# Halves of the rotated features exchanged by small loads in chip memory instead of a product with a permutation

## The chip, the cores and the metric

One core of one Trainium2 chip runs the whole program in one launch. The time is the device time of that launch in microseconds (us). TensorE multiplies, VectorE and ScalarE work on tiles, GpSimd does small work beside them, and SP (the sync engine) issues all loads and stores. Everything is float32; the large products are made in three passes from rounded parts.

## What is computed

Three layers on 512 positions of 1,024 features: an attention over a sliding window of 128 with one sink per head, a stick-breaking attention, and a hybrid mixer (convolution and state space), each with a gated feed-forward part. The change concerns the first attention, of 16 query heads and 2 key heads of 64 features:

```python
q = partial_rope(rmsnorm(q, q_gain), positions)
k = partial_rope(rmsnorm(k, k_gain), positions)
...
x1, x2 = xr[..., :half], xr[..., half:]
rot = jnp.concatenate([x1 * cos - x2 * sin, x2 * cos + x1 * sin], axis=-1)
return jnp.concatenate([rot, x[..., ROT_DIM:]], axis=-1)
```

Only the first 16 of the 64 features of a head are turned (`half` is 8), so every turned feature needs the one that stands 8 further on or back.

## The kernel before

Features lie on the 128 partitions, positions (512) along the row. A query tile holds two heads, at partitions 0 to 63 and 64 to 127; there are eight query tiles and one tile of keys, "k". `score()` writes one list of steps (ticks), and every engine runs through the same list and does its own part of each step, in that order, so the order of work is written out by hand. Signals (semaphores) tie the engines together; `Waits.wait_ge` leaves out waits that are already known to hold.

Weights come as a stream of 361 units of 512 KB (eight blocks of 128 by 128): SP loads one into one of three `raw` buffers (L1892) once VectorE is done with the unit that was there, ScalarE makes its upper part (`cut`, L1128), VectorE its lower part (L1420), and TensorE makes three products for each block (L755, L757, L759). Beside it SP loads the modulation weights (L1905, 512 KB each, six buffers), and VectorE multiplies and adds them (L1428, L1431); such a load waits for the multiply-add that frees its buffer.

The first attention, 66 to 176 us of the profiled execution, is a pipeline woven into the products of the queries' own projection and, later, of the output projection. For a tile `t`, the step `query` (for the keys `kstat` and `krope`) does this:

- ScalarE, when the product of the tile is done: square into `QSQ`, and the tile times its gain into `QG` (L1208, L1209), one of five buffers.
- TensorE: sums of squares (`head_stats`, L876), then the product of `QG` with a permutation matrix, which exchanges rows 0 to 7 with 8 to 15 and rows 64 to 71 with 72 to 79 and leaves zero elsewhere (`turn_halves`, L884), each into a bank of its own.
- VectorE: the statistics out of the bank (L1601), `QG` times the cosines (L1611), the permuted tile times the signed sines into `qt` (L1615), and the sum (L1617). GpSimd takes the power -1/2 of the statistics (L1833).

For the keys, `kspread` spreads the statistics over the rows (L902) and VectorE scales the keys with it (L1622); the values are transposed (L910). Then the pipeline has four stages for each half of a tile: `scores` (L927; VectorE adds the mask and takes maxima, L1645), `exps` on ScalarE (L1287), `turned` (transposes, L941) and `values` (L955, L965, then L1672 on VectorE). In one round the list has `scores` of a new half, `query` of the next tile, and the later stages of earlier halves.

The eight banks of PSUM are handed round in turn: `take` pops the bank that was given longest ago and waits for what was to be done with it, `give` puts it back at the end of the row. From `query` of tile 6 on, four of the eight are held by results of the output projection.

```python
def take(key):
    i, sig, by = free.popleft()
    if sig is not None:
        w.wait_ge(sig, by)
    bank_of[key] = i
    return psum[i]
```

## Time and profile before

| | |
|---|---|
| median of 3 runs | 2362.5 us (2361.22 to 2362.77) |
| profiled execution | 2362.4 us |
| its span | 2360.6 us |
| TensorE busy | 2302.7 us (98%) |
| VectorE busy | 1168.1 us (49%) |
| ScalarE busy | 870.8 us (37%) |
| GpSimd busy | 155.1 us (7%) |
| mean granted clock of TensorE | 0.991 |

The span runs from the first to the last instruction of the profiled execution; its own time also has what lies around the span. A busy TensorE is not a TensorE at its peak, since matmuls overlap and their ends are modelled; starts are safer than ends. A wait is shown with the instruction behind it and with what ended it. The granted clock is a share of 2.4 GHz.

### The profile page before, as it was taken

The numbers are of one execution on the slowest core, as the hardware profiler recorded it, in microseconds if no ns is written. First come the engines' busy times: TensorE is split into PE (matmuls) and PEld (weight loads), VectorE is DVE, ScalarE is ACT, GpSimd is POOL, SyncE is SP. The second block draws the span as 40 slices with busy tenths as digits, with TensorE's granted clock in tenths as the row PEclk, the third lists the DMA queues.
The fourth block names the chain that finished last, engine by engine and source line by source line (L and its number), as shares of the span: only waits on it lengthen the run. The fifth ranks groups of instructions, "written<-read, shape, count | busy, mean of one in ns | idle before, by whom it ended". The sixth has DMA issues, their size and how long they took to land.

```text
span 2360.6 us, 27446 instructions
## 1 busy us (share of the span) xinstructions
PE 2302.7 (98%) x11216; PEld 1842.1 (78%) x11216; DVE 1168.1 (49%) x1615; ACT 870.8 (37%) x1413; POOL 155.1 (7%) x145
## 2 busy tenths in 40 slices
PE   8999999999999999999999999999999999999998
PEld 6767788888777677888887877866778887888886
DVE  3765665543465744333335455556743345553453
ACT  3554322132354533322323236356363223332332
POOL 1111000000100010000010002022020001000001
PEclk9999999999999999999999999999999999999999
DMA  9323465522212122222232222211223222233222
GB/s 318 134 99 111 175 216 202 207 98 98 81 63 72 46 71 83 96 98 98 90 107 81 98 90 98 98 55 63 72 90 107 98 81 98 87 101 106 92 88 81
DMA packets 77518, 250.69 MB, mean 106 GB/s; under 512 B 8272, under 2 KB 16720, under 8 KB 77392
## 3 DMA queue, kind: packets, MB, share of 16 engines
q1 hardware_dynamic: 77392, 248.93, 30.4%
q8 instruction: 89, 1.46, 0.3%
q14 instruction: 37, 0.30, 0.0%
HBM read 244.70 MB, written 4.19 MB: 105 GB/s over the span
## 4 chain that ended last, share of the span: by engine, by line
PE 82%; ACT 3%; DVE 3%; issue 1%; POOL 1%; POOLq 0%; DVEq 0%; ACTq 0%
PE pb L755 25%; PE pb L759 24%; PE pb L757 24%; PE pb L979 1%; PE pb L1004 1%; PE pb L989 1%; PE pb L1073 1%; DVE slab L1684 1%; PE pb L779 1%; PE pb L775 1%; PE pb L777 1%; PE pb L1054 1%; PE pb L800 0%; PE pb L861 0%; ACT slab L1381 0%
## 5 line engine op out<-in xcount | busy, mean ns | idle before, releaser
L755 PE MATMUL pb<-hhi,whi 128*128 128x512 f32 x1976 | 787.0, 398 | 4.2 <-ACT hhi L1156 2.4
L1420 DVE TENSOR_TENSOR wlo<-raw,whi 128x1024 fp32r<-128x1024 f32 x361 | 449.1, 1248 | 686.9 <-ACT whi L1128 686.9
L757 PE MATMUL pb<-hhi,wlo 128*128 128x512 f32 x1976 | 771.3, 390 | 1.7 <-DVE wlo L1420 1.7
L759 PE MATMUL pb<-hlo,whi 128*128 128x512 f32 x1976 | 771.4, 390 | 0.4 <-DVE hlo L1416 0.4
L1128 ACT ACTIVATE whi<-raw 128x1024 fp32r<-128x1024 f32 x361 | 379.2, 1056 | 688.8 <-PE pb L759 672.0
L755 PEld LDWEIGHTS pb<-hhi,whi 128*128 128x128 f32 x1976 | 371.2, 188 | 98.5 <-issue 24.5
L759 PEld LDWEIGHTS pb<-hlo,whi 128*128 128x128 f32 x1976 | 371.2, 188 | 81.8 <-DVE hlo L1416 1.6
L757 PEld LDWEIGHTS pb<-hhi,wlo 128*128 128x128 f32 x1976 | 371.7, 188 | 78.8 <-DVE wlo L1420 2.7
L755 PE MATMUL pb<-ahi,whi 128*128 128x512 f32 x848 | 336.2, 396 | 1.4 <-ACT ahi L1310 0.7
L759 PE MATMUL pb<-alo,whi 128*128 128x512 f32 x848 | 331.3, 391 | 0.0
L757 PE MATMUL pb<-ahi,wlo 128*128 128x512 f32 x848 | 331.2, 391 | 0.0
L755 PEld LDWEIGHTS pb<-ahi,whi 128*128 128x128 f32 x848 | 159.9, 189 | 39.2 <-issue 6.1
L759 PEld LDWEIGHTS pb<-alo,whi 128*128 128x128 f32 x848 | 159.7, 188 | 34.5 <-DVE alo L1416 0.8
L757 PEld LDWEIGHTS pb<-ahi,wlo 128*128 128x128 f32 x848 | 159.9, 189 | 32.7 <-issue 0.7
L1842 POOL TENSOR_TENSOR slab<-slab 128x512 f32<-128x512 f32 x44 | 62.0, 1410 | 1588.2 <-ACT slab L1145 1587.3
L1511 DVE SCALAR_TENSOR_TENSOR slab<-slab,vec 128x509 f32<-128x509 f32 (+2 forms) x132 | 99.0, 750 | 4.7
L1416 DVE TENSOR_TENSOR alo<-slab,ahi 128x512 fp32r<-128x512 f32 x90 | 62.3, 692 | 67.9 <-ACT ahi L1227 50.4
L1431 DVE SCALAR_TENSOR_TENSOR slab<-slab,small 128x1024 f32<-128x1024 f32 x70 | 89.9, 1284 | 1.9
L1145 ACT ACTIVATE slab<-X 128x512 f32<-128x512 f32 x48 | 30.3, 632 | 109.3 <-PE pb L759 39.5
L1684 DVE TENSOR_TENSOR_SCAN slab<-slab,cst 128x128 f32<-128x128 f32 (+3 forms) x64 | 52.5, 820 | 31.0 <-ACT slab L1323 31.0
L1542 DVE TENSOR_TENSOR slab<-slab,pb 128x512 f32<-128x512 f32 x66 | 45.0, 682 | 43.6 <-PE pb L759 43.6
L1227 ACT ACTIVATE ahi<-slab 128x512 fp32r<-128x512 f32 x66 | 41.7, 632 | 66.0 <-DVE slab L1542 65.8
(232 smaller groups left out, 1702.9 us busy)
## 6 DMA issues: line engine op xcount, KB each, us to landing
raw<-stream SPq DMA_DIRECT2D x361, 512.0 KB, 3.3
slab<-ada_w SPq DMA_DIRECT2D x80, 512.0 KB, 5.0
early<-ada_w SPq DMA_DIRECT2D x32, 256.0 KB, 7.6
X<-xT SPq DMA_DIRECT2D x8, 256.0 KB, 4.5
ya<-slab SPq DMA_DIRECT2D x8, 256.0 KB, 2.3
slab<-ya SPq DMA_DIRECT2D x8, 256.0 KB, 4.9
outT<-X SPq DMA_DIRECT2D x8, 256.0 KB, 2.1
cst<-consts SPq DMA_DIRECT2D x1, 576.0 KB, 7.2
```

What stands on the lines that cost most here:

```text
L755: e.matmul(out, wh, hi, start=s.k == 0, stop=False)
L757: e.matmul(out, wl, hi, start=False, stop=False)
L759: i = e.matmul(out, wh, lo, start=False, stop=s.last)
L1128: e.activation(whi[:, u % NW, :], raw[:, u % NRAW, :], ACT.Copy).then_inc(*a_cut.up(u))
L1227: e.activation(a_out[f % HALF][0], SG[f % 6], ACT.Copy).then_inc(*a_half.up(("f", l, f)))
L1416: e.tensor_tensor(out, src, hi.bitcast(F), ALU.subtract).then_inc(*v_half.up(key))
L1420: e.tensor_tensor(wlo[:, u % NW, :], raw[:, u % NRAW, :], whi[:, u % NW, :].bitcast(F), ALU.subtract).then_inc(*v_cut.up(u))
L1431: e.scalar_tensor_tensor(o, a, cond[:, k:k + 1], o, ALU.mult, ALU.add).then_inc(*v_mod.up(("fma", n)))
L1511: e.scalar_tensor_tensor(t[:, d:], u[:, :S - d], W(name, (width - 1 - d) * tiles + i), t[:, d:], ALU.mult, ALU.add).then_inc(*v_conv.up((k ...
L1542: e.tensor_tensor(t, t, b, ALU.mult).then_inc(*v_ev.up(tile))
L1684: e.tensor_tensor_scan(p[:, 0:wd][:, ::-1], RS[n % 4][:, 0:wd][:, ::-1], C("late", S - wd)[:, 0:wd][:, ::-1], 1.0, ALU.mult, ALU.max).then ...
L1842: e.tensor_tensor(acc, acc, sq_of(sid, d), ALU.add).then_inc(*p_sum.up((sid, d)))
```

## The change

The product with the permutation goes, with its bank, for all nine tiles. In its place a buffer `swapped` (slot 46, which the first attention did not use) is cleared once by GpSimd, and SP fills its 32 rows that matter with four loads from `QG`, eight rows of 2 KB each, at the steps `krope` and `query`. Before it issues them SP waits for the clearing, for ScalarE's `QG`, and for VectorE's product with the sines of the tile before, which reads the same buffer. VectorE's product with the sines waits for the fourth load and reads `swapped` in place of the bank. The order of work on VectorE stays.

```diff
+    d_swap = signal("d_swap", 16)
...
-    qt = slot(21)
+    qt, swapped = slot(21), slot(46)
...
-        def turn_halves(t):
-            b = take(("rope", t))
-            w.wait_ge(d_late, "in")
-            w.wait_ge(a_ev, ("qkv", qn(t) + 7 if t == "k" else t) if t != "k" else ("qkv", 8))
-            e.matmul(b, C("perm"), QG[qn(t) % 5], start=True, stop=True).then_inc(*t_att.up(("rope", t)))
-            give(("rope", t), v_att, ("rope2", t))
...
-        def query(t):
-            head_stats(t)
-            turn_halves(t)
...
-            w.wait_ge(t_att, ("rope", t))
+            w.wait_ge(d_swap, (t, 3))
             if t != "k":
                 w.wait_ge(v_att, ("rope", t - 1 if t else "k"))
-            e.tensor_tensor(qt, bank(("rope", t)), sinT, ALU.mult).then_inc(*v_att.up(("rope2", t)))
+            e.tensor_tensor(qt, swapped, sinT, ALU.mult).then_inc(*v_att.up(("rope2", t)))
...
+        def tables():
+            w.wait_ge(t_mod, ("pre", 3))
+            e.memset(swapped, 0.0).then_inc(*p_rope.up("blank"))
...
+        def swap(t):
+
+            w.wait_ge(p_rope, "blank")
+            w.wait_ge(a_ev, ("qkv", 8 if t == "k" else t))
+            if t != "k":
+                w.wait_ge(v_att, ("rope2", t - 1 if t else "k"))
+            for n, (to, of) in enumerate(((0, 8), (8, 0), (64, 72), (72, 64))):
+                e.dma_start(swapped[to:to + 8, :], QG[qn(t) % 5][of:of + 8, :]).then_inc(*d_swap.up((t, n)))
...
-        do = {"cut": lambda u: load() if u > 2 else None, "fma": fma, "evac": evac, "fetch": fetch, "final": final}
+        do = {"cut": lambda u: load() if u > 2 else None, "fma": fma, "evac": evac, "krope": lambda: swap("k"), "query": swap, "fetch": fetch, "final": final}
```

SP's queue around the keys and the first tiles, before: L1892 loads a unit of the weight stream, L1905 modulation weights.

```order
L1892 DMA raw<-stream 128x1024 [waits v_cut]
L1905 DMA slab<-ada_w 128x1024 [waits v_mod] x4
L1892 DMA raw<-stream 128x1024 [waits v_cut] x2
L1905 DMA slab<-ada_w 128x1024 [waits v_mod] x2
L1892 DMA raw<-stream 128x1024 [waits v_cut]
L1905 DMA slab<-ada_w 128x1024 [waits v_mod]
```

The same place with the change: L1886 and L1899 are these two lines, L1914 is the exchange (`spare_74` is `swapped`).

```order
L1899 DMA slab<-ada_w 128x1024 [waits v_mod] x4
L1914 DMA spare_74<-slab 8x512 [waits a_ev,p_rope]
L1914 DMA spare_74<-slab 8x512 x3
L1914 DMA spare_74<-slab 8x512 [waits v_att,a_ev]
L1914 DMA spare_74<-slab 8x512 x3
L1886 DMA raw<-stream 128x1024 [waits v_cut]
L1914 DMA spare_74<-slab 8x512 [waits v_att,a_ev]
L1914 DMA spare_74<-slab 8x512 x3
L1886 DMA raw<-stream 128x1024 [waits v_cut]
L1899 DMA slab<-ada_w 128x1024 [waits v_mod] x2
L1914 DMA spare_74<-slab 8x512 [waits v_att,a_ev]
L1914 DMA spare_74<-slab 8x512 x3
```

The exchanges of the keys and of tile 0 stand behind four loads of modulation weights, that of tile 1 behind one load of the stream, that of tile 2 behind one of the stream and two of modulation weights; the next load of the stream comes behind each.

TensorE at the same place, before: two sums of squares (L876), each with a permutation (L884), between products of the projection.

```order
L759 MATMUL pb<-hlo,whi 128x512
L876 MATMUL pb<-cst,slab 128x2 x4
L884 MATMUL pb<-slab,cst 128x512
L876 MATMUL pb<-cst,slab 128x2 x4
L884 MATMUL pb<-slab,cst 128x512
L755 MATMUL pb<-hhi,whi 128x512
L757 MATMUL pb<-hhi,wlo 128x512
L759 MATMUL pb<-hlo,whi 128x512
```

And with the change (L877 is L876; L756, L758 and L760 are L755, L757 and L759):

```order
L760 MATMUL pb<-hlo,whi 128x512
L877 MATMUL pb<-cst,slab 128x2 x8
L756 MATMUL pb<-hhi,whi 128x512
L758 MATMUL pb<-hhi,wlo 128x512
L760 MATMUL pb<-hlo,whi 128x512
```

The two statistics stand together and the products of the projection follow at once.

## Rows read from the trace of the kernel before

**Rows 1.** Page, part 4: shares of the chain that ended last, by engine.

```profile
PE 82%; ACT 3%; DVE 3%; issue 1%; POOL 1%; POOLq 0%; DVEq 0%; ACTq 0%
```

**Rows 2.** Busy time by stretches; at the end clock, DMA share, GB/s.

```profile
50.00:100.00 50.00, 47.22 (x265) 34.92 (x264) 37.81 (x86) 24.60 (x53) 8.03 (x4) 0.97 0.50 177
100.00:150.00 50.00, 50.00 (x397) 38.63 (x396) 32.81 (x109) 33.95 (x91) 6.03 (x3) 1.00 0.24 86
150.00:200.00 50.00, 42.03 (x305) 32.02 (x305) 26.00 (x81) 25.98 (x73) 4.02 (x2) 0.93 0.24 85
```

**Rows 3.** Line of the permutation: min/median/max ns, first and last start.

```profile
L884 PE MATMUL pb<-slab,cst x16: 592/634/676, 67.8 to 174.5; 128*128 128x512 f32 x16
```

**Rows 4.** TensorE in order of time: start, us, engine, line, operation.

```profile
75.47 1.93 PE L902 MATMUL pb<-cst,small 128*64 128x128 f32 x16 [2.78 <-POOL small L1833]
...
81.45 0.93 PE L927 MATMUL pb<-slab 64*128 64x128 f32 x8
...
85.17 0.95 PE L876 MATMUL pb<-cst,slab 128*128 128x2 f32 x8
85.99 1.10 PE L884 MATMUL pb<-slab,cst 128*128 128x512 f32 x2
87.02 1.14 PE L927 MATMUL pb<-slab 64*128 64x256 f32 x8
```

**Rows 5.** VectorE in order of time, the start of the attention.

```profile
67.80 5.44 DVE L1431 SCALAR_TENSOR_TENSOR slab<-slab,small 128x1024 f32<-128x1024 f32 x4
73.16 0.16 DVE L1601 TENSOR_SCALAR small<-pb 128x8 f32<-128x8 f32 x1
...
73.84 0.68 DVE L1615 TENSOR_TENSOR slab<-pb,slab 128x512 f32<-128x512 f32 x1
...
77.44 0.69 DVE L1622 TENSOR_TENSOR slab<-slab,pb 128x512 f32<-128x512 f32 x1 [0.19 <-PE pb L902]
```

**Rows 6.** SP's issues in order of time: start us, us, how many.

```profile
1.64 0.42 SPq L1928 DMA_DIRECT2D pos<-positions  x1
...
68.29 3.93 SPq L1905 DMA_DIRECT2D slab<-ada_w  x4
...
92.86 0.91 SPq L1905 DMA_DIRECT2D slab<-ada_w  x2
...
135.16 0.81 SPq L1905 DMA_DIRECT2D slab<-ada_w  x2
...
153.80 0.43 SPq L1905 DMA_DIRECT2D slab<-ada_w  x1
```

**Rows 7.** DMA issues, KB each, us to landing: 82:88, then 0:20.

```profile
raw<-stream SPq DMA_DIRECT2D x1, 512.0 KB, 3.1
...
pos<-positions SPq DMA_DIRECT2D x1, 2.0 KB, 2.3
```

**Rows 8.** Stretches of half a us, then DMA strips of 92:100 and 153:159.

```profile
76.50:77.00 0.50, 0.50 (x10) 0.50 (x6) 0.47 (x2) 0.00 (x0) 0.50 (x1) 0.50 0.85 344
77.00:77.50 0.50, 0.50 (x5) 0.17 (x2) 0.31 (x2) 0.00 (x0) 0.42 (x1) 0.50 0.21 82
...
DMA  0000000974999998999989998989521000000000
...
DMA  0000000008979989999999989685432100000000
```

**Rows 9.** VectorE's product with the sines, tiles 2, 5 and 6.

```profile
96.62 0.69 DVE L1615 TENSOR_TENSOR slab<-pb,slab 128x512 f32<-128x512 f32 x1
...
139.93 0.68 DVE L1615 TENSOR_TENSOR slab<-pb,slab 128x512 f32<-128x512 f32 x1
...
155.19 0.68 DVE L1615 TENSOR_TENSOR slab<-pb,slab 128x512 f32<-128x512 f32 x1
```

**Rows 10.** TensorE's first products with the values, tiles 4 and 5; wait in brackets.

```profile
157.69 1.55 PE L955 MATMUL pb<-slab 128*64 128x128 f32 x12 [1.10 <-DVE small L1645]
...
177.65 0.88 PE L955 MATMUL pb<-slab 128*64 128x128 f32 x12 [0.45 <-DVE small L1645]
```

More of the change, by code:

```diff
@@ L1085, in tensor @@
               "tables": tables, "kstat": lambda: head_stats("k"),
-              "krope": lambda: turn_halves("k"), "kspread": kspread, "vturn": vturn, "query": query, "scores": scores, "turned": turned,
+              "kspread": kspread, "vturn": vturn, "query": head_stats, "scores": scores, "turned": turned,
               "values": values, "start": start, "turn": turn, "gather": gather, "dtturn": dtturn, "xrow": xrow, "bturn": bturn,
@@ L1872, in decay @@
             e.tensor_tensor(ex[:, P:], ex[:, P:], Ct[g % 2][:, P:], ALU.mult).then_inc(*p_ssd.up(("ex", g, h)))
-        do = {"angles": angles, "pow": pow_, "kstat": lambda: head_pow("k"), "query": head_pow, "sq": sq,
+        def tables():
+            w.wait_ge(t_mod, ("pre", 3))
+            e.memset(swapped, 0.0).then_inc(*p_rope.up("blank"))
+        do = {"angles": angles, "tables": tables, "pow": pow_, "kstat": lambda: head_pow("k"), "query": head_pow, "sq": sq,
               "evac": evac, "state": state, "decay": decay}
@@ L1946, in program @@
     engines = tensor, scalar, vector, gpsimd, sync
-    signals = [d_in, d_pos, d_out, *d_x, *d_raw, *d_ada, *d_early.values(), d_late, *d_ya, t_mm, t_mod, t_norm, t_att, t_stick, t_ssd, a_cut, a_half,
+    signals = [d_in, d_pos, d_out, *d_x, *d_raw, *d_ada, *d_early.values(), d_late, d_swap, *d_ya, t_mm, t_mod, t_norm, t_att, t_stick, t_ssd, a_cut, a_half,
                a_ev, a_sq, a_att, a_stick, a_ssd, v_cut, v_half, v_ev, v_mod, v_norm, v_res, v_att, v_stick, v_ssd, v_conv, p_sum,
```

## The prediction, made before the changed kernel had run

> **What bounds the kernel now.** The page first. The chain of waits that ended last is 82% TensorE [rows 1], so what counts is time in which TensorE works or waits. The change touches only the attention of the first layer, 66 to 176 us, so I read busy time by stretches next: TensorE is busy 50.00 of 50 us from 100 to 150, but only 42.03 from 150 to 200 [rows 2]. In the middle, a product less is time gained. At the two ends of the pipeline TensorE waits for others, and there it is not. The granted clock says the same: 1.00 in the middle, 0.97 and 0.93 around it. Since its two levels are 2.4 and 1.2 GHz, 0.97 of 50 us is 3.0 us at half clock and 0.93 is 7.0 us; one dip costs about 1.5 us of work.
>
> Then the line that goes. Nine products with the permutation take two passes of some 0.63 us each [rows 3] (eight of them; the ninth reads another buffer). What one occupies is read from starts: the one of tile 1 starts at 85.99, the scores behind it at 87.02, so 1.03 us [rows 4].
>
> **The change, part by part.** Time runs from the profiled execution, 2362.4 us for a span of 2360.6; the median of the three runs is 2362.5, so the same.
>
> Removed, tiles 1 to 5: five products of 1.03 us in the stretch without idle time, 5.15 us gained if the new wait stays hidden.
>
> Removed, keys and tile 0: nothing. After them TensorE waits 2.78 us at 75.47 for GpSimd's power of the key statistics [rows 4], and that hangs on VectorE, which is busy with multiply-adds (5.44 us from 67.80) and takes the key statistics only at 73.16 [rows 5]. Two products less make this wait 4.8 us instead of 2.8. The half clock behind it (0.50, [rows 8]) is there already.
>
> Added: 36 loads of 8 rows by 2 KB on SP, four for each tile, and VectorE's wait for the fourth. No row shows such a load. An issue is bounded by nothing below and by 0.42 us above, which the 2 KB of positions took [rows 6]; I take 0.42, since a load of as few bytes took it. Landing: 2.3 us for that one, 3.1 us for a 512 KB weight load alone [rows 7]; I take 2.3 and keep 2.0 to 3.8 for the range, the upper end because writes from chip memory to chip memory have no row. So a quartet lands 3 x 0.42 + 2.3 = 3.56 us after SP gets to it, at best.
>
> When SP gets to it is the second question. SP is released by VectorE's splits and multiply-adds, so before each exchange it has just issued one to four loads of 512 KB, which stand ahead of it in the same queue.
>
> Keys: SP has issued its fourth modulation load by 68.29 + 3.93 = 72.22 [rows 6]; by itself the exchange would land at 75.8. But the transfers ahead run until about 77.2: share 0.85 and then 0.21 in two half microseconds [rows 8]. I take 77.4. VectorE wanted the turned keys at 73.84 [rows 5]. Tile 0's exchange may start only when the product with the sines of the keys is done (one buffer for all), 0.69 us later at 78.1, and lands at 78.1 + 3.56 = 81.65. Behind it stand that product, the sum and the scaling of the keys, with the pitches of the trace 0.72 + 0.60 + 0.69 = 2.0, so the keys are ready at 83.65 where they were at 77.44 + 0.69 = 78.13 [rows 5]. TensorE wants them at 81.45 [rows 4], as now, since its order up to there starts from 75.47. Stall: 83.65 - 81.45 = **+2.2 us**.
>
> Tile 2: SP is free at 92.86 + 0.91 = 93.77 [rows 6], three loads of 512 KB ahead run out at about 98.0 [rows 8], in the first strip with slices of 0.2 us, so the exchange lands at 98.2 and VectorE wanted it at 96.62 [rows 9]. It waits 1.6 us, but has some microseconds of slack behind it; for TensorE 0, at most 1.
>
> Tile 5, the closest of the others: free after the first of the two loads, which share 0.81 us from 135.16, at 135.58 [rows 6] (the second now comes behind the exchange), landing 139.1 against 139.93 [rows 9]. Hidden. Tiles 1, 3, 4 and 7 have 1 us or more.
>
> Tile 6: SP free at 153.80 + 0.43 = 154.23 [rows 6]; transfers ahead end at about 157.4 [rows 8], in the second strip with slices of 0.15 us, own landing 157.8. VectorE wanted it at 155.19 [rows 9], so everything behind it on VectorE comes 2.6 us later, the score maxima of tile 5 first. TensorE stands at exactly these: the bank for the output of tile 4 comes free with them, and it waits for that until 157.69 [rows 10]. With the banks handed round in turn and two takings fewer a tile, this bank's releaser stays the same. So **+2.6 us**, and the saved product is only more waiting. At tile 7 the same pair stands a little apart (wait 0.45 us [rows 10], exchange long landed): about 0.2 gained.
>
> GpSimd's one clearing of the buffer lies long before 72 us. VectorE's product reads chip memory instead of a bank: same duration within 0.01 us. Bytes: 9 x 64 KB, nothing beside 512 KB loads.
>
> Sum: 2.2 - 5.15 + 2.6 - 0.2 = -0.55 us, **2361.9 us**.
>
> The row for positions is a load on an idle queue. The Trainium skill, "DMA: Bandwidth & Descriptors", section "Anatomy of one DMA", gives 2.0 us fixed plus bytes over 436 GB/s for one transfer, fitted for another way of issuing, so an estimate of 2.04 us here. By that price in place of 2.3 the exchanges of tile 0 and tile 6 land 0.26 us sooner (that of the keys waits for the transfers ahead all the same), and the sum would be -1.1 us.
>
> **Rivals.** (a) *The exchange does not queue behind the large loads.* For it: 8 rows need not travel over the same engines as 128. Then the exchange of the keys lands at 75.8, the product behind it ends at 76.5, that of tile 0 lands at 80.1, the keys are ready at 82.1, stall 0.65; tile 6 unchanged, since its own 3.56 us decides. Sum -2.1 us: 2360.3. Against it: a 512 KB load behind another takes longer to land, as its transfers come in turn. The Trainium skill, same page, section "Queues, rings and completion order", says that each engine consumes one ring's descriptors in ring order; by that rule (a) falls, and the sum stays -0.55.
>
> (b) *Issues of 8 rows cost 0.1 us and land in 2.0 us.* Then 2.3 us in place of 3.56 each time: keys 74.5, tile 0 at 77.5, no stall at the start, tile 6 late by 1.35. Sum -5.15 + 1.35 - 0.2 = -4.0: 2358.4. If tile 6 is hidden as well, -5.35: 2357.0, the most that can be had. Against it: positions took 0.42 us although tiny.
>
> (c) *The exchange becomes the wait*, on the slow side. If four chip-memory loads land in 3.8 us instead of 2.3, tile 0's comes 1.5 us later, the stall before the first scores is 3.7 us, longer than the wait of 2.78 us after which the clock is at half [rows 4, 8]. That is 1.5 us, and 1.5 more for a dip. Tile 6 pays 1.5 more, tiles 3 and 5 pass their margins for some 0.7. Sum -0.55 + 5.2 = +4.65: 2367.0, and more with each further tenth. For it: two exchanges in series stand at the start with nothing between them, and the dependence on one buffer. It decides from a landing of about 3.8 us.
>
> **How the numbers follow.** A measurement of this kernel tells 0.2%, 4.7 us, from no change. Chances: forecast 0.45, (a) 0.20, (b) 0.15, (c) 0.20. Forecast and (a) are within the bound; (b) goes past it about half of the time, and so does (c) with most of its chance: faster 0.10, same 0.71, slower 0.19. The range runs from just below (b), 2358.0, to just past the edge of (c), 2367.5.
>
> **What would show it.** Right: no line of the permutation on TensorE; 36 loads of 16 KB from SP; VectorE idle before its product with the sines some 3.5 us at the keys and 2 to 4 at tile 0, 1.6 at tile 2, 2.6 at tile 6, nothing elsewhere; TensorE's first scores start about 2 us later than 81.45, their successors catch up 1.03 a tile, and the output of tile 4 loses it again. Wrong: waits before the sines at every tile (landing above 3.8 us), a second half-clock stretch right after 83 us, or weight loads late behind the exchanges so that ScalarE's splits wait for data.

## The result and the profile after

| | before | with the change |
|---|---|---|
| median, same chips | 2361.45 us (2355.9 to 2363.8, 10 runs) | 2367.11 us (2363.5 to 2372.37, 10 runs) |
| mean of these runs | 2361.14 us | 2367.97 us |
| ratio, 95% interval | | 1.0029 (1.0019 to 1.0039) |
| profiled execution, span | 2362.4, 2360.6 us | 2371.81, 2370.0 us |
| its granted clock | 0.991 | 0.987 |

The change makes the kernel slower by 0.29%, above the 0.2% that can be told from no change. The forecast was no difference, 2361.9; what came is rival (c), and nearly its number, 2367.0. The profiled execution lies at the slow end of the ten runs (they spread with the granted clock, 2363.5 at 0.991 and 2372.37 at 0.987), so its 9.4 us must not be read as the cost; the means say 6.8. Of all runs further down one, of the version "early", took 2898.55 us at a granted clock of 0.746; it is left out.

The page first, the busy time of TensorE and the shares of the chain of waits. The chain has the shares of [rows 1], and TensorE is busy 2.5 us less in a span that is 9.4 us longer.

```profile
PE 2300.2 (97%) x11198; PEld 1844.4 (78%) x11198; DVE 1168.1 (49%) x1615; ACT 870.2 (37%) x1413; POOL 155.5 (7%) x146
...
PE 82%; ACT 3%; DVE 3%; issue 1%; POOL 1%; POOLq 0%; DVEq 0%; ACTq 0%
```

SP's issues in order of time, the counterpart of [rows 6] (start us, us, how many). ada_w are the modulation weights and `spare<-slab` is the exchange.

```profile
67.81 3.93 SPq L1899 DMA_DIRECT2D slab<-ada_w  x4
71.86 10.19 SPq L1914 DMA_DIRECT2D spare<-slab  x8
...
157.18 2.65 SPq L1914 DMA_DIRECT2D spare<-slab  x4
```

A quartet takes 2.65 us of SP, not 1.7 (the two of keys and tile 0 stand in one row, with the wait between them). The entry of the changed kernel's line L1914: min/median/max ns of one issue, and who waited for the landings, us and times:

```profile
L1914 SPq DMA_DIRECT2D spare<-slab x32: 624/625/772, 71.9 to 176.1; - x32
...
  DVE slab L1605: 15.6, 6
```

0.62 us for 16 KB, where 512 KB of the stream take 0.33; with the gap from one to the next the pitch is 0.67 us. VectorE in order of time in the changed kernel, the rows that waited most for a load, all of the product with the sines (L1605 is L1615 of [rows 5, 9]); in brackets the idle time before and what ended it:

```profile
78.64 0.69 DVE L1605 TENSOR_TENSOR slab<-spare,slab 128x512 f32<-128x512 f32 x1 [5.19 <-DMA spare<-slab]
...
83.47 0.69 DVE L1605 TENSOR_TENSOR slab<-spare,slab 128x512 f32<-128x512 f32 x1 [2.74 <-DMA spare<-slab]
...
105.49 0.69 DVE L1605 TENSOR_TENSOR slab<-spare,slab 128x512 f32<-128x512 f32 x1 [2.83 <-DMA spare<-slab]
...
161.64 0.69 DVE L1605 TENSOR_TENSOR slab<-spare,slab 128x512 f32<-128x512 f32 x1 [3.53 <-DMA spare<-slab]
```

These are the keys and tiles 0, 2 and 6; tiles 4 and 5 waited 0.76 and 0.54 us. Tile 0's last load starts at 71.86 + 10.19 - 0.62 = 81.43 and lands at 83.47, 2.0 us later; tile 6's starts at 157.18 + 3 x 0.67 = 159.19 and lands at 161.64, 2.4 us later. These landings are near the forecast, the issue is not. The keys' last load starts at 74.02 and lands 4.6 us later, at 78.64. The packets of the trace show why (a packet is a piece of a load as one DMA engine moves it): those of the keys' exchange, 32 of 2 KB, start from 75.91 to 77.66 us, behind nearly all of those of the four large loads issued before them. At tile 6, where two loads of 512 KB stand ahead, they start only at 160.14, 3.0 us after SP's first issue; at tile 0, where nothing stands ahead, at 80.69. TensorE in order of time, which answers to [rows 4]:

```profile
75.09 1.98 PE L896 MATMUL pb<-cst,small 128*64 128x128 f32 x16 [4.34 <-POOL small L1823]
...
85.63 1.65 PE L917 MATMUL pb<-slab 64*128 64x128 f32 x8 [4.74 <-DVE slab L1612]
...
87.80 0.63 PE L758 MATMUL pb<-hhi,wlo 128*128 128x512 f32 x1
...
93.02 1.13 PE L917 MATMUL pb<-slab 64*128 64x256 f32 x8
```

And the first product with the values of tile 4, which answers to [rows 10]:

```profile
164.15 1.55 PE L945 MATMUL pb<-slab 128*64 128x128 f32 x12 [5.92 <-DVE small L1635]
```

The first scores wait 4.74 us and start at 85.63 instead of 81.45, and take 1.65 us instead of 0.93: half clock. So do the products behind them (0.63 instead of 0.39 each) up to 91.6. The scores of tile 0 and 1 at 93.02 stand where those of 87.02 stood, 6.0 us later. Between them and tile 6 the lag falls by 0.94 to 0.97 us a tile, but for a new wait of 0.60 at tile 2. The first product with the values of tile 4 waits 5.92 us instead of 1.10. Busy time by stretches in the changed kernel, columns as in [rows 2]:

```profile
50.00:100.00 50.00, 40.84 (x213) 31.11 (x212) 31.73 (x65) 20.30 (x42) 6.55 (x4) 0.90 0.44 148
100.00:150.00 50.00, 49.40 (x413) 39.78 (x413) 37.18 (x125) 35.45 (x98) 8.04 (x4) 1.00 0.35 120
150.00:200.00 50.00, 37.74 (x253) 28.96 (x249) 23.86 (x72) 24.30 (x66) 4.02 (x2) 0.83 0.17 58
```

In the middle TensorE is still busy nearly throughout at full clock. At the ends it is idle more, and the clock is 0.90 and 0.83 where it was 0.97 and 0.93.

The second end goes on behind the row at 164.15. The first product with the values of tile 5 ([rows 10]) starts at 186.19:

```profile
186.19 0.88 PE L945 MATMUL pb<-slab 128*64 128x128 f32 x12 [1.13 <-DVE small L1635]
```

The same stretch, from tile 4's to tile 5's, before and then with the change:

```profile
157.69:177.65 19.96, 16.82 (x106) 12.72 (x106) 8.92 (x32) 8.57 (x24) 2.01 (x1) 0.83 0.22 80
...
164.15:186.19 22.04, 18.22 (x103) 14.23 (x103) 8.83 (x32) 8.80 (x24) 2.01 (x1) 0.71 0.23 75
```

It is 2.1 us longer, at a granted clock of 0.71 instead of 0.83. Stretches of half a us around the landing of the keys, as in [rows 8]; the number before the last is the DMA share:

```profile
77.50:78.00 0.50, 0.50 (x4) 0.50 (x3) 0.00 (x0) 0.00 (x0) 0.00 (x0) 0.50 0.18 66
...
80.50:81.00 0.50, 0.40 (x2) 0.00 (x0) 0.23 (x1) 0.50 (x1) 0.50 (x1) 1.00 0.18 33
```

An exchange alone shows a share of 0.18 (80.5 to 81, tile 0's), and so does the tail from 77.5 to 78, in which the last of the keys' packets run beside the last few of the large loads.

### The profile page after: what moved, and what is told of

Same layout as the page of the kernel before. It is cut to its first block, busy times and chain, and to the rows that moved or that the text cites. A ratio compares the mean times of both kernels' runs of the same rounds, so it can differ in the third digit from the quotient of the medians.

```text
span 2370.0 us, 27456 instructions
## 1 busy us (share of the span) xinstructions
PE 2300.2 (97%) x11198; PEld 1844.4 (78%) x11198; DVE 1168.1 (49%) x1615; ACT 870.2 (37%) x1413; POOL 155.5 (7%) x146
## 4 chain that ended last, share of the span: by engine, by line
PE 82%; ACT 3%; DVE 3%; issue 1%; POOL 1%; POOLq 0%; DVEq 0%; ACTq 0%
PE pb L756 24%; PE pb L758 24%; PE pb L760 24%; PE pb L969 1%; PE pb L994 1%; PE pb L979 1%; PE pb L1063 1%; PE pb L776 1%; DVE slab L1674 1%; PE pb L780 1%; PE pb L778 1%; PE pb L1044 1%; PE pb L801 0%; PE pb L854 0%; PE pb L862 0%
## 5 line engine op out<-in xcount | busy, mean ns | idle before, releaser
L756 PE MATMUL pb<-hhi,whi 128*128 128x512 f32 x1976 | 787.4, 398 | 4.6 <-ACT hhi L1146 2.7
L758 PE MATMUL pb<-hhi,wlo 128*128 128x512 f32 x1976 | 771.7, 391 | 1.7 <-DVE wlo L1410 1.7
L760 PE MATMUL pb<-hlo,whi 128*128 128x512 f32 x1976 | 772.4, 391 | 0.4 <-DVE hlo L1406 0.4
L756 PEld LDWEIGHTS pb<-hhi,whi 128*128 128x128 f32 x1976 | 371.9, 188 | 98.9 <-issue 24.3
L760 PEld LDWEIGHTS pb<-hlo,whi 128*128 128x128 f32 x1976 | 371.4, 188 | 82.2 <-DVE hlo L1406 1.6
L758 PEld LDWEIGHTS pb<-hhi,wlo 128*128 128x128 f32 x1976 | 372.2, 188 | 78.3 <-DVE wlo L1410 2.7
L756 PE MATMUL pb<-ahi,whi 128*128 128x512 f32 x848 | 336.9, 397 | 1.4 <-ACT ahi L1300 0.7
L760 PE MATMUL pb<-alo,whi 128*128 128x512 f32 x848 | 331.5, 391 | 0.0
L758 PE MATMUL pb<-ahi,wlo 128*128 128x512 f32 x848 | 331.5, 391 | 0.0
L756 PEld LDWEIGHTS pb<-ahi,whi 128*128 128x128 f32 x848 | 160.1, 189 | 39.3 <-issue 6.3
L760 PEld LDWEIGHTS pb<-alo,whi 128*128 128x128 f32 x848 | 160.0, 189 | 34.9 <-DVE alo L1406 0.8
L758 PEld LDWEIGHTS pb<-ahi,wlo 128*128 128x128 f32 x848 | 160.3, 189 | 32.6 <-issue 0.7
```

What stands on the lines that cost most here:

```text
L756: e.matmul(out, wh, hi, start=s.k == 0, stop=False)
L758: e.matmul(out, wl, hi, start=False, stop=False)
L760: i = e.matmul(out, wh, lo, start=False, stop=s.last)
```

## The experiments

Eleven edits of the changed kernel ran, one of them twice, timed beside the kernel before; ratios and the column of means compare with its runs in the same job. Each expectation names its theories in its own words; common to them is theory 1, that the exchange comes late at the start and at tile 6, with a half clock behind the first scores as its second part, against rivals by which another cost (the weight loads, the clock alone, the middle tiles) makes the loss. Of long lines the cuts of code show only the part that changes. Three lengths in each trace tell most. **a** is from the start of the product that spreads the key statistics (75.47 in [rows 4]) to the first scores, which holds the stall at the start. **b** is from there to the first product with the values of tile 4 (157.69 in [rows 10]), which holds the products of tiles 1 to 5, a half clock behind the scores, and the wait at tile 6. **c** is from there to the first product with the values of tile 5 (177.65 in [rows 10]), which holds the half clock behind that wait; its granted clock stands in brackets. The spreading product itself starts at 74.8 to 77.3 in these traces, and a, b and c leave that out. Each length is read from one execution.

| | median (range), runs | mean less before's | ratio to before, 95% | a | b | c | wait of tile 4's values | clock of first scores |
|---|---|---|---|---|---|---|---|---|
| before | in each job its own | | | 5.98 | 76.24 | 19.96 (0.83) | 1.10 | full |
| the change | 2367.11 (2363.5 to 2372.37), 10 | +6.83 | 1.0029 (1.0019 to 1.0039) | 10.54 | 78.52 | 22.04 (0.71) | 5.92 | half |
| none | 2352.9 (2351.56 to 2360.94), 12 | -5.85 | 0.9974 (0.9962 to 0.9987) | 5.70 | 71.40 | 18.19 (0.91) | 2.30 | full |
| own0 | 2362.02 (2357.93 to 2370.45), 11 | +1.39 | 1.0007 (0.9995 to 1.002) | 7.33 | 75.74 | 19.00 (0.86) | 5.84 | full |
| warm | 2364.66 (2361.66 to 2371.75), 12 | +4.99 | 1.0022 (1.0011 to 1.0034) | 9.97 | 75.59 | 19.72 (0.83) | 6.07 | full |
| six | 2364.74 (2359.19 to 2369.3), 12 | +3.73 | 1.0013 (1.0003 to 1.0024) | 11.63 | 74.09 | 19.34 (0.85) | 2.30 | half |
| own0six | 2360.32 (2353.4 to 2362.67), 12 | -0.92 | 0.9998 (0.9986 to 1.001) | 8.47 | 72.01 | 20.86 (0.75) | 2.30 | full |
| early | 2365.30 (2361.75 to 2366.22), 11 | +3.83 | 1.0017 (1.0006 to 1.0027) | 11.31 | 74.19 | 19.78 (0.83) | 2.30 | half |
| start | 2360.24 (2358.2 to 2365.12), 12 | +0.24 | 1.0002 (0.9991 to 1.0013) | 6.29 | 75.80 | 22.11 (0.71) | 5.86 | full |
| all | 2352.5 (2351.58 to 2360.56), 12 | -6.74 | 0.9971 (0.9959 to 0.9982) | 5.77 | 71.40 | 18.16 (0.91) | 2.30 | full |
| one | 2363.01 (2358.37 to 2367.36), 12 | +2.31 | 1.0012 (1.0001 to 1.0024) | 8.64 | 74.51 | 19.25 (0.85) | 5.27 | full |
| act_queue | 2363.79 (2361.72 to 2369.89), 12 | +3.85 | 1.0017 (1.0006 to 1.0028) | 8.38 | 73.77 | 21.24 (0.82) | 2.30 | full |
| rows16 | 2368.31 (2365.35 to 2371.65), 11 | +7.11 | 1.0026 (1.0017 to 1.0035) | 10.96 | 79.93 | 18.84 (0.87) | 6.55 | half |

The lengths of "early" are from a trace of its own, "early_look". Summed up, a, b and c less before's agree with the difference of the means within 2.1 us in every row but that of "act_queue" (+1.2 against +3.85), so a difference of 2 us between two rows needs both the times and the rows behind it. Part of a is chance: in the seven versions that issue the keys' exchange where the change does, it landed 3.0 ("warm") to 4.7 us ("six") after the start of the spreading product, 3.55 in the changed kernel.

**None: the exchange and its wait left out.**

```diff
-            w.wait_ge(d_swap, (t, 3))
+            w.wait_ge(p_rope, "blank")
...
-"krope": lambda: swap("k"), "query": swap, "fetch": fetch
+"fetch": fetch
```

> The changed kernel with the 36 exchange loads and VectorE's wait for them left out, so the product with the sines reads zeros (the turned halves are missing). It is the change's gain without its waits. Theory 1 (the loss is the late exchange at the start and at tile 6): seven products of 1.03 us less, two of them swallowed at tile 6 and 7, so -5.2 to -5.5 us against the kernel before, ratio 0.9978; first scores at 81 us as before, no half clock after them. Theory 2 (the loss comes from the other order of bank releases and from the clock, whatever the exchange does): this kernel is not faster than before, ratio 1.000 or more, and the dip after the first scores stays.

TensorE in this kernel, in order of time, at the output of tile 4:

```profile
152.04 0.88 PE L945 MATMUL pb<-slab 128*64 128x128 f32 x12 [2.30 <-DVE small L1635]
```

Without the exchange the change is a gain of 9.4 us by the medians (2352.9 against 2362.29 in the same job), 5.85 by the means; the means are safer, since the runs of both kernels fall into groups by their granted clock. Length b is 4.84 us shorter than before: five products. The sixth, of tile 6, shows in the wait, which is 2.30 instead of 1.10. That is the saved product that "is only more waiting". The product with the values then runs at full clock (0.88 us, 1.55 in [rows 10]), and the half clock comes just behind it (0.50 from 153 to 154). But c is 1.8 us shorter, at a granted clock of 0.91 instead of 0.83: a gain that the sum had no term for. The other order of the banks, the rival here, is in this kernel too, and yet it is faster than the one before; so the whole loss comes from the exchange, 12.7 us by the means.

**Own0: tile 0's exchange in a buffer of its own**, so that it needn't wait for VectorE's product with the sines of the keys. Each tile also has a semaphore of its own here, as in "own0six", "start" and "all".

```diff
+                e.dma_start((swapped0 if t == 0 else swapped)[to:to + 8, :], QG[qn(t) % 5][of:of + 8, :]).then_inc(*d_swaps[t].up((t, n)))
...
-            if t != "k":
+            if t not in ("k", 0):
                 w.wait_ge(v_att, ("rope2", t - 1 if t else "k"))
```

> The changed kernel with a buffer of its own for tile 0's exchange, issued at its old place but without waiting for VectorE's product with the sines of the keys. If the two exchanges in series are the larger half of the late start: tile 0's quartet is issued from 74.5 to 77.2, it is there when VectorE comes to it at 80, VectorE waits for it 0.5 us at most instead of 2.7, the first scores start near 83 instead of 85.6 after a wait of 2 us, and the half clock behind them may go: 2.5 us less than the changed kernel without it, 5.5 with. If the landing of the keys' exchange behind the large loads sets the start: less than 1 us.

VectorE in this kernel waits once at the start, for the keys:

```profile
77.93 0.69 DVE L1605 TENSOR_TENSOR slab<-spare,slab 128x512 f32<-128x512 f32 x1 [4.81 <-DMA spare<-slab]
```

TensorE's first scores:

```profile
82.09 0.93 PE L917 MATMUL pb<-slab 64*128 64x128 f32 x8 [1.52 <-DVE slab L1612]
```

Length a falls by 3.21 us, and with a wait of 1.52 us instead of 4.74 ahead of them the first scores run at full clock: b falls by 2.78. The mean comes down by 5.4 us. So the two exchanges in series, with the half clock that their wait brings, are the larger part of the loss; 0.4 of the 3.2 us of a is only that the keys landed earlier in this trace.

**Warm: the stall kept, TensorE kept at work in it.** Four products with the identity, whose result nobody reads, stand ahead of the wait.

```diff
             b = [take(("s", t, pair, h)) for h in range(2)]
+            if (t, pair) == (0, 0):
+                for _ in range(4):
+                    e.matmul(b[0], ident, cst[:, 0:S], start=True, stop=True)
```

> The changed kernel with four more products of 128 by 512 with the identity on TensorE, into the bank of the first scores, ahead of its wait for the keys; they fill 4.1 of the 4.7 us it stands there. Theory 1a (part of the loss is the half clock that follows this wait): no half clock from 85 to 91.6, so 2.5 to 3 us less than the changed kernel, 2364.5. Theory 1b (the waits alone are the loss, the clock only reports them): the same as the changed kernel or up to 0.5 us more, 2367.

TensorE in this kernel, the added products (L913) and the scores behind them:

```profile
81.31 3.59 PE L913 MATMUL pb<-cst 128*128 128x512 f32 x8
85.41 0.93 PE L920 MATMUL pb<-slab 64*128 64x128 f32 x8 [0.51 <-DVE slab L1615]
```

The scores start as late as before this edit (85.41), but at full clock (0.93 us), and b is 2.93 us shorter, with 0.26 less waiting at tile 2 and 0.15 more at tile 6. That leaves 2.8 us as the price of the half clock behind the first scores, apart from the stall. The times agree with it but don't show it by themselves: the mean comes down by 1.8, the median by 2.45, and the two intervals overlap.

**Six: the exchanges of tiles 6 and 7 alone one tile earlier.**

```diff
-"query": swap, "fetch": fetch
+"query": lambda t: [swap(i) for i in {5: (5, 6), 6: (7,), 7: ()}.get(t, (t,))], "fetch": fetch
```

> The changed kernel, with the exchanges of tiles 6 and 7 alone issued one tile earlier (behind those of tiles 5 and 6). Theory 1 (the late exchange at tile 6 is a term of its own, paid besides the start): no wait for a load before the product with the sines of tile 6, the product for the output of tile 4 starts 4 to 5 us after its start in the changed kernel less 4.6, so about 159.5 us instead of 164.15, and the time falls from about 2368 by 4 to 6 us to 2362 to 2364, about the kernel before; the start stays late (first scores near 85.6). Rival (the wait of VectorE at tile 6 only fills time that TensorE would lose anyway to the bank of tile 4): the start of that product and the time stay within 1 us of the changed kernel's.

SP in this kernel, the exchanges of tiles 5 and 6 in one row:

```profile
139.20 8.06 SPq L1914 DMA_DIRECT2D spare<-slab  x8
```

TensorE at the output of tile 4:

```profile
160.60 1.55 PE L945 MATMUL pb<-slab 128*64 128x128 f32 x12 [2.30 <-DVE small L1635]
```

The wait for tile 6 on VectorE is gone, and TensorE's falls from 5.92 to the 2.30 us of "none": the late exchange costs 3.62 us there, all of it TensorE's. Length b falls by 4.43, the mean by 3.1 (4 to 6 had been expected). The rival, that this wait only fills time lost anyway, is out. Length a is 1.1 longer in this trace, since the keys landed that much later.

**Own0six: both.** The edits of the last two together.

> The same move of tiles 6 and 7, and tile 0's exchange into a buffer of its own, at its old place behind that of the keys. Theory 1 (the two lateness terms add): first scores near 82.1, output of tile 4 near 153 instead of 157.83, time 2355 to 2358, faster than the kernel before by 0.2% or more, with waits left only at tiles 2 and 4. Rival (the moves of tiles 1 to 5 are what makes the version with every move fast): 2360 or more.

TensorE at the output of tile 4:

```profile
156.71 0.88 PE L945 MATMUL pb<-slab 128*64 128x128 f32 x12 [2.30 <-DVE small L1635]
```

Both terms are gone (b = 72.01), and the time is that of the kernel before, 0.9998 (0.9986 to 1.001); the forecast of 2355 to 2358 was too low by 2 to 5 us, and the number is the rival's. The rival's reason is not what the trace shows: tiles 1 to 5 still cost TensorE only 0.54 us, at tile 2. What is left is the start and the clock. The keys' own exchange lands at 80.54 after a wait of 5.95 us, a is 8.47 where the version "all", below, has 5.77. It accounts for 2.7 of the 5.8 us between the means of the two (2359.71 and 2353.93) and tile 2 for 0.5. Another 2.7 us stand in c, 20.86 at a clock of 0.75 against 18.16 at 0.91: more half clock behind the output of tile 4, though the wait ahead of it is 2.30 us in both. Why it fell so here stays open.

**Early, and early_look: the exchanges of tiles 1 to 7 one tile earlier**, those of the keys and of tile 0 in their place.

```diff
+            if tile == ("qkv", 1):
+                swap(1)
...
-"query": swap, "fetch": fetch
+"query": lambda t: swap(0) if t == 0 else swap(t + 1) if t < 7 else None, "fetch": fetch
```

> The changed kernel with the exchanges of tiles 1 to 7 issued one tile earlier on SP (right after VectorE's product with the sines of the tile before, ahead of the weight loads); keys and tile 0 stay. Theory 1: VectorE's waits at tiles 2, 4, 5 and 6 (2.8, 0.8, 0.5, 3.5 us in the trace) go, the wait of TensorE before the output of tile 4 falls from 5.9 us to about 2, the start stays late by 4.2 us and at half clock after it. So 5 to 6 us less than the changed kernel, 0 to +1 us against before, ratio 1.000. Theory 2: no shorter than the changed kernel, ratio 1.003.

> A second look at the kernel with the exchanges of tiles 1 to 7 one tile earlier, whose profiled execution was at a granted clock of 0.746 throughout. Expected in its rows: first scores at 85.6 and a half clock after them as in the changed kernel, no wait of VectorE for an exchange from tile 1 on, and 2.3 us of TensorE's wait before the output of tile 4, as in the kernel without exchange.

SP at the start of this kernel:

```profile
74.05 15.82 SPq L1916 DMA_DIRECT2D spare<-slab  x12
89.91 0.44 SPq L1886 DMA_DIRECT2D raw<-stream  x1
```

VectorE's wait at tile 0:

```profile
86.43 0.69 DVE L1605 TENSOR_TENSOR slab<-spare,slab 128x512 f32<-128x512 f32 x1 [2.76 <-DMA spare<-slab]
```

And the first scores:

```profile
88.59 1.65 PE L917 MATMUL pb<-slab 64*128 64x128 f32 x8 [5.29 <-DVE slab L1612]
```

No tile from 1 on waits for its load any more. But the load of the stream now stands behind tile 1's exchange, which waits for VectorE, and is issued at 89.91; and the start is as bad as in the changed kernel (a = 11.31, half clock). The wait at tile 6 is gone as in "six", and the gain is the same, 3.0 us by the means where 5 to 6 had been expected: moving the other tiles adds nothing that shows while the start stays.

**Start: the exchanges of the keys and tile 0 right behind ScalarE's write**, tile 0 in its own buffer; tiles 1 to 7 as in the change.

```diff
         def evac(tile):
+            if tile in (("qkv", 8), ("qkv", 0)):
+                swap("k" if tile[1] else 0)
...
-"krope": lambda: swap("k"), "query": swap, "fetch": fetch
+"query": lambda t: swap(t) if t else None, "fetch": fetch
```

> The changed kernel with the exchanges of the keys and of tile 0 issued right after ScalarE has written each (between the modulation loads), tile 0 into a buffer of its own; tiles 1 to 7 stay. Theory 1: the first scores start at 81.1 instead of 85.6 and no half clock follows, 6 us less than the changed kernel; tile 6 still costs 4.6 us and its dip. Against before -1 to +1 us, ratio 1.000. If the loads wait behind large transfers however early they are issued, the keys land at 76 or later and the start keeps 2 us of its 4.2.

SP in this kernel, the exchange of the keys and the one large load ahead of it:

```profile
68.03 0.46 SPq L1900 DMA_DIRECT2D slab<-ada_w  x1
68.61 2.88 SPq L1917 DMA_DIRECT2D spare<-slab  x4
```

TensorE's first scores:

```profile
81.60 0.93 PE L917 MATMUL pb<-slab 64*128 64x128 f32 x8 [0.48 <-DVE slab L1612]
```

One large load of four stands ahead of the keys' exchange now, and a is 6.29, within 0.3 us of before, with the clock full. The mean comes down by 6.6 us. What remains is tile 6, with a wait of 5.86 us (b = 75.80).

**All: both moves**, the edit of "start" with this for the other tiles:

```diff
+            if tile in (("qkv", 8), ("qkv", 0), ("qkv", 1)):
+                swap("k" if tile[1] == 8 else tile[1])
...
+"query": lambda t: swap(t + 1) if 0 < t < 7 else None, "fetch": fetch
```

> Both moves together: every exchange issued as soon as its data and buffer are there. Theory 1: as without exchange, -5 us against before, ratio 0.998, and VectorE waits for no exchange at all. Theory 2: ratio 1.002 or more. If SP's 2.65 us for each quartet delay the weight loads instead, ScalarE's splits wait for data and the gain is below 2 us.

VectorE's waits for a load in this kernel, all there are:

```profile
73.97 0.69 DVE L1605 TENSOR_TENSOR slab<-spare,slab 128x512 f32<-128x512 f32 x1 [0.50 <-DMA spare<-slab]
...
78.32 0.69 DVE L1605 TENSOR_TENSOR slab<-spare,slab 128x512 f32<-128x512 f32 x1 [2.26 <-DMA spare<-slab]
```

TensorE at the output of tile 4:

```profile
152.28 0.88 PE L945 MATMUL pb<-slab 128*64 128x128 f32 x12 [2.30 <-DVE small L1635]
```

The stretch that has the second end of the pipeline, columns as in [rows 2]:

```profile
150.00:200.00 50.00, 40.29 (x311) 31.17 (x312) 24.90 (x81) 24.87 (x65) 3.37 (x2) 0.97 0.24 90
```

The exchange is hidden from TensorE: a and b are those of "none" within 0.1 us, and the median, 2352.5, within 0.4. VectorE was expected to wait for no exchange at all and still waits for two, which costs TensorE nothing that shows. The clock of the last stretch is 0.97, where it was 0.93 before: of its two half-clock stretches one is gone, as in "none" (c is 18.16), and the other begins at 153, behind the row above. This version computes everything and is faster than both kernels, 0.9971 (0.9959 to 0.9982) of the one before.

**One: a single load of 8 rows for each tile** in place of four; three quarters of the turned halves are missing.

```diff
-            for n, (to, of) in enumerate(((0, 8), (8, 0), (64, 72), (72, 64))):
+            for n, (to, of) in enumerate(((0, 8),)):
```

> The changed kernel with one load of 8 rows for each tile instead of four (the other three exchanges are left out, so three quarters of the turned halves are missing). Theory 'issue' (SP's 0.62 us for each such load is what was mis-sized, 2.65 us a quartet): tile 0's and tile 6's exchange land 2.0 us sooner, the first scores start 2 us earlier, TensorE's wait before the output of tile 4 is 3.9 us instead of 5.9; 4 us less than the changed kernel, and up to 2.8 more if the dip at the start goes. Theory 'queue' (they land late because they stand behind 512 KB loads): no more than 1 us less, the waits at the keys and tile 6 stay.

SP in this kernel, the four large loads and the first two exchanges:

```profile
69.24 3.93 SPq L1899 DMA_DIRECT2D slab<-ada_w  x4
73.28 8.36 SPq L1914 DMA_DIRECT2D spare<-slab  x2
```

VectorE's waits at the keys and tile 0:

```profile
80.23 0.69 DVE L1605 TENSOR_TENSOR slab<-spare,slab 128x512 f32<-128x512 f32 x1 [5.36 <-DMA spare<-slab]
...
83.00 0.69 DVE L1605 TENSOR_TENSOR slab<-spare,slab 128x512 f32<-128x512 f32 x1 [0.67 <-DMA spare<-slab]
```

SP and VectorE at tile 6:

```profile
152.81 0.43 SPq L1899 DMA_DIRECT2D slab<-ada_w  x1
153.34 0.65 SPq L1914 DMA_DIRECT2D spare<-slab  x1
...
157.16 0.69 DVE L1605 TENSOR_TENSOR slab<-spare,slab 128x512 f32<-128x512 f32 x1 [2.88 <-DMA spare<-slab]
```

With three issues fewer tile 0 waits 0.67 us instead of 2.74, and a falls by 1.9. The keys do not gain: their only load starts at 73.28 and lands at 80.23, 6.9 us later. Nor does tile 6, by much: its only load lands 3.8 us after its issue, where the four took 4.5 from the first issue, and TensorE's wait there is 5.27 us, not the 3.9 that was expected if the issue were the price. So at tile 0 the four issues are the cost; at the keys and at tile 6 it is the large loads ahead. The time fell by 4.5 us by the means, where the theory of the issue said 4, and up to 6.8 if the half clock at the start went. It did go, behind a wait of 2.62 us, and most of b's fall of 4.0 us is that.

**Act_queue: the exchanges issued by ScalarE instead of SP.** The function moves unchanged into ScalarE's part, at the same steps.

```diff
+              "krope": lambda: swap("k"), "query": swap, "vturn": vturn, "start": start, "turn": turn,
```

> The changed kernel with the exchanges issued from ScalarE's queue at the same steps, same waits. ScalarE is idle from 68 to 78 us, so the keys' exchange goes out at 69 and is there when VectorE wants it, tile 0's follows its product with the sines and lands 4 us later: first scores at 82 to 83 instead of 85.6. At tile 6 ScalarE reaches the step at about 157 as well, but its loads do not stand behind SP's: if another queue passes the large loads, VectorE waits 1 us less there. ScalarE pays 2.65 us of issuing a tile, which must not reach TensorE for this to hold: 2361 to 2364. If it reaches TensorE, 2368 or more with waits of TensorE for ScalarE's exponentials.

ScalarE in this kernel (ACTq is its queue of issues):

```profile
68.91 1.23 ACTq L1309 DMA_DIRECT2D spare<-slab  x1
...
70.17 11.81 ACTq L1309 DMA_DIRECT2D spare<-slab  x7
82.02 0.60 ACT L1313 ACTIVATE slab<-pb 128x512 f32<-128x512 f32 x1 [11.81 <-issue]
```

The four large loads on SP:

```profile
70.00 3.93 SPq L1908 DMA_DIRECT2D slab<-ada_w  x4
```

VectorE's waits at the keys and tile 0:

```profile
78.24 0.69 DVE L1614 TENSOR_TENSOR slab<-spare,slab 128x512 f32<-128x512 f32 x1 [2.60 <-DMA spare<-slab]
...
83.50 0.69 DVE L1614 TENSOR_TENSOR slab<-spare,slab 128x512 f32<-128x512 f32 x1 [3.17 <-DMA spare<-slab]
```

An issue costs ScalarE the same, 0.63 us, and the seven that follow the first, with their wait, keep it from its other work for 11.81 us. The keys' first load is issued at 68.91 in another queue, before SP issues the four large ones at 70.00 to 73.93, and yet it lands at 78.24, 4.3 us behind SP's last issue (6.9 in the changed kernel: 78.64 - 71.74). Its packets start from 70.37 to 77.42, among those of the large loads, which run on to 80. So another queue helps by a part and doesn't pass the large loads, and the first scores do not come at 82 to 83, as expected, but at 85.66. By the means it stands 3.85 us over before; waits of 0.4 to 2.7 us appear at tiles 1 to 5, none at tile 6. Lengths a and b do not hold that cost (together they are those of before); 1.8 us of it stand ahead of them, where the spreading product starts at 77.28, and 1.3 in c.

**Rows16: four loads of 16 rows**, copied to their own place; nothing is exchanged.

```diff
-            for n, (to, of) in enumerate(((0, 8), (8, 0), (64, 72), (72, 64))):
-                e.dma_start(swapped[to:to + 8, :], QG[qn(t) % 5][of:of + 8, :]).then_inc(*d_swap.up((t, n)))
+            for n, (to, of) in enumerate(((0, 0), (16, 16), (64, 64), (80, 80))):
+                e.dma_start(swapped[to:to + 16, :], QG[qn(t) % 5][of:of + 16, :]).then_inc(*d_swap.up((t, n)))
```

> The changed kernel with four loads of 16 rows for each tile in place of four of 8 (rows copied to their own place, so the halves are not exchanged). If 0.62 us is the price of a load of few rows, it issues in 0.33 us like the weight loads, a quartet in 1.5 us instead of 2.65, and tile 0 and tile 6 come 1.1 us sooner each: 2 us less than the changed kernel, 2365. If 0.62 us is the price of a load from chip memory to chip memory, nothing changes: 2367.

The entry of the issuing line in this kernel, min/median/max ns:

```profile
L1914 SPq DMA_DIRECT2D spare<-slab x32: 507/589/1451, 73.4 to 178.7; - x32
```

VectorE's wait at tile 6:

```profile
165.04 0.69 DVE L1605 TENSOR_TENSOR slab<-spare,slab 128x512 f32<-128x512 f32 x1 [4.16 <-DMA spare<-slab]
```

An issue of twice the rows takes 0.59 us at the median, a little less than one of 8, so it is not priced by the bytes; 128 rows from device memory take 0.33. The landing is longer: the last issue of tile 6 starts at 159.95 + 2.41 - 0.59 = 161.77 and lands at 165.04, 3.3 us later against 2.4. The time is that of the changed kernel, 2368.31 and 2367.11.

## Why the prediction was wrong

The places were right, and all three that cost time were named: the start, tile 2 and tile 6. Two steps failed: the price of an exchange, which made the wait at the start too short by half, and the clock behind that wait, which was put at nothing and which rival (c) had.

**Products saved.** Forecast five of 1.03 us, 5.15; measured 4.84 ("none", length b). Right, and also that those of the keys and tile 0 are worth nothing (a is 5.70 without them against 5.98) and that of tile 6 only lengthens a wait.

**The price of an exchange, the first step that failed.** "An issue is bounded by nothing below and by 0.42 us above, which the 2 KB of positions took": it is 0.62 us, with a pitch of 0.67. A load of one row of positions was taken as the upper end for a load of eight rows between buffers, though the text itself says that no row shows such a load. The landing of 2.3 us held where nothing or little was ahead (2.0 and 2.4), so a quartet took 4.0 us at tile 0 and 4.5 at tile 6 from its first issue, not 3.56. By itself this is worth 0.6 us at the start and at most 0.9 at tile 6; with it put right the sum would have come to about +1 us, still no difference that can be told.

**The start.** Forecast +2.2, measured 10.54 - 5.98 = +4.56, so 2.4 more. Tile 0's chain gives 83.47 - 78.64 = 4.83 from one product with the sines to the next where 0.69 + 3.56 = 4.25 were reckoned: 0.6. The keys landed at 78.64, not 77.4: 1.2. The rest is the head of the kernel, 0.38 earlier in this trace, and 0.2 on VectorE. The 77.4 was the end of the transfers ahead with next to nothing for the exchange's own; its packets ran to 77.74 here, and VectorE was released 0.9 us after that. The rule that settled rival (a), from the Trainium skill's page "DMA: Bandwidth & Descriptors", section "Queues, rings and completion order", held here: the exchange came behind the large loads (78.64), also with one load only (80.23). An exchange from another queue is late too ("act_queue"), which that rule doesn't settle.

**The half clock behind the first scores, the second step that failed and the largest.** Forecast 0, measured 2.8 to 2.9 us ("warm" and "own0", length b). The forecast held that a stall of 2.2 us would leave the clock alone; at 4.74 us the clock was at half for 6 us. A second half-clock stretch right after 83 us was one of the forecast's own signs of being wrong, and it came. In the other traces too the scores ran at half clock behind waits of 4.95 us ("rows16") to 5.82 ("six"), and at full clock behind waits up to 2.62 ("one").

**Tile 2.** Forecast 1.6 us on VectorE and 0 to 1 on TensorE; measured 2.83 and 0.60. **Tile 6.** Forecast +2.6, measured 5.92 - 2.30 = +3.62: SP was free at 157.08, and 4.5 us stood there from the first issue to the landing in place of 3.56. The forecast held that the exchange's own time decides there; "one" shows that it is mostly the two large loads ahead, since a single load took 3.8. **Behind tile 6** the sum had no term: c is 2.1 us longer, and with a wait of nearly the same length it was 19.00 ("own0") or 22.11 ("start"), so one trace doesn't give its price.

Put together, to the output of tile 4: 4.56 - 4.84 + 2.8 + 0.60 + 3.62 = +6.7 us. The trace has (10.54 + 78.52) - (5.98 + 76.24) = +6.84. That the means also say +6.83 is in part chance, since c adds 2.1 in this trace, which is one of the slower executions. The places and the queue were right; the sum missed by 2.4 at the start, 2.8 for the clock, 1.0 at tile 6 and 0.6 at tile 2, all to the same side.

**The rivals.** (a) fell: the exchange does queue. (b) fell: an issue is not 0.1 us. Its keys at 74.5 also left out the queue, which by [rows 8] ran until 77.2. (c) came true in its mechanism, a longer wait at the start with a half clock behind it, though not by the cause it named: it wanted a landing of 3.8 us, and the landing was 2.0 to 2.4 behind dearer issues and a later end of the large loads. Its number, 2367.0, was met by luck. It stands 4.65 us over 2362.4, while the difference of the means is 6.83 and the kernel before ran at 2361.45 this time; its dip was 1.5 and measured 2.8. Both bounds that were open, issue and landing, pointed the same way, since neither had a row of its own kind.

## What to carry to other kernels

A load within chip memory is no cheap stand-in for a product: here four of 16 KB took SP 2.65 us and 4.0 to 4.5 us until the data were there, for 1.03 us of TensorE. It paid when it was issued a whole tile ahead, ahead of most of the large loads in its queue, and with a second buffer where two exchanges follow each other at once: the same change, so placed, went from 0.29% slower to 0.29% faster. Look first for transfers in series through one buffer, and price a stall of TensorE with the half clock behind it.

## What the runs showed of the hardware

- Issuing a load of 8 rows of 2 KB between buffers takes 0.62 us on SP and 0.63 on ScalarE, one of 16 rows 0.59, while 128 rows of 4 KB from device memory take 0.33. The count of bytes doesn't explain it; what does was not tried.
- Such a load landed 2.0 us after its issue with nothing ahead of it, 2.4 (the last of four) and 3.8 (one alone) behind two loads of 512 KB, and 4.6 to 6.9 behind four. By the Trainium skill's page "DMA: Bandwidth & Descriptors", section "Anatomy of one DMA", 16 KB would be about 2.04 us, an estimate from a fit for another way of issuing; the trace of the free case agrees. The same order of SP in two versions ("start" and "all") gave the keys at 76.32 and 73.97: this spread stays open.
- One stall of 4.74 us ahead of the scores cost 2.8 us more behind it. With the wait filled by four products that nobody reads, 3.59 us altogether, the half clock did not come.
- Issued from ScalarE's queue, the keys' exchange ran among the large loads of SP's queue (its packets from 70.37 to 77.42) and landed 4.3 us behind their last issue, against 6.9 from SP's own queue.
- The runs of one kernel spread by 9 us and more (12.5 for "own0"), and with the granted clock: the changed kernel from 2363.5 at 0.991 to 2372.37 at 0.987. So 0.001 of the mean clock goes with about 2.2 us, and a single execution can mislead by more than this change cost.
